# Inverse roots of two norms: Ln and Exp on ScalarE replaced by an addition and a power on GpSimd

## The chip, the cores and the metric

The kernel runs on one core of a Trainium2 chip. The metric is device microseconds of one execution, as the median of several. A core has TensorE (PE in the profile, with its weight loads as PEld), VectorE (DVE), ScalarE (ACT), GpSimd (POOL) and SyncE (SP, which issues most DMAs). Each engine runs its own list of instructions strictly in order, and engines wait for each other with semaphores.

## The reference

Two transformer-like blocks in float32 over 1024 tokens of width 1024, with 16 meta tokens in front. What matters here is the middle of the first block, where two mixers run side by side:

- `hgrn2_mixer` (the recurrence): 6 heads of 64, a gated linear recurrence. Its output `o` is normed for each token and head: `o * rsqrt(mean(o*o) + 1e-6)`, then times a weight and a gate.
- `mamba2_mixer` (the chunks): 6 heads of 64 in 2 groups, done in chunks. Its output `y`, times a gate, is normed for each token over each group of 192: `y * rsqrt(mean(y*y) + 1e-6)`, then times a weight.

After them come a third mixer (already done by then), the output projection, layer norms, two feed-forward parts and a second block, all outside the change.

## The kernel before

The program is written once for each engine (`tensor_program`, `scalar_program`, `vector_program`, `gpsimd_program`, `sync_program`), as a row of stages. The stage of this change is `weave(..._hgrn, ..._ssd)` on each engine. It starts when the projections are done (about 430 us into the span) and ends where the output projection begins (about 716 us).

Each `_hgrn` and `_ssd` function is a Python generator that emits instructions between `yield`s. `weave` takes one step of each generator in turn, hgrn first. So the order of instructions on each engine is fixed when the program is built, by the number of yields, and nothing is reordered on the chip.

- hgrn works on three pairs of heads, i = 0, 1, 2 (`pairs`: at most two live, each starting 9 turns after the one before). A pair runs 17 steps: gates and a scan, the transposes and states, then 7 levels of score products (steps 4 to 12), then the outputs in two halves h = 0, 1 (steps 13 to 16). In steps 13 and 14 ACT copies the outputs of a half out of PSUM and squares them into `S.SQ`. DVE sums the squares for each head into `S.SS[h]` (128x8) in steps 14 and 15 (`squares`), then needs `S.RS[h]`, the inverse root, to scale the outputs (`gated`, steps 15 and 16). PE then transposes them into `YA`.
- ssd works on nine chunks, r = 0 to 8 (`ssd_chunks`: at most two live, chunk r+1 starts in the turn in which chunk r is at step 5, or one earlier). In step 5 DVE finishes `S.Y[x]`, and ACT squares its two groups with an accumulated sum into `S.SSB[x]` (128x2). DVE scales by the inverse root in step 6 (`normed`), and PE transposes it in step 7. Chunk 0 has no norm.

Before the change ACT makes the inverse root itself, with Ln (scale 1/64 or 1/192, bias `k.eps`) and then Exp with scale -0.5: in `root(h)` for the recurrence, in line in `act_ssd` for the chunks. That is 6 roots of 128x8 and 8 of 128x2. The Ln and the Exp are each preceded by a load of an activation table. The other functions of the stage on ACT are Exp, Copy, Relu, Square and Abs, and at the start of a pair one Ln and one Sigmoid.

Behind the root of a chunk in ACT's order stand the decay rows of the next chunk (`gaps`, `decay`), the exponentials of hgrn's levels (`level exp`) and copies of score products out of PSUM, which free the bank in which PE puts the next product.

GpSimd in this stage: `XDD` (128x384, step 1 of a chunk, needed by PE for the state), half of the decayed score product `m2(r, 1)` (128x384, step 3), and per pair the products `QG` (step 1) and `gate` (step 12), both 128x1024. In later stages it makes the roots of the layer norms and of the second block's norm as a power: `g.tt(rs, rs, k.mhalf.to_broadcast(...), ALU.pow)`, with `k.mhalf` a column of -0.5.

Of the kernel before, what the change touches and what calls it, by code (L numbers as in the profile page):

```python
# [9 lines left out]
ALU = mybir.AluOpType  # L10
ACT = mybir.ActivationFunctionType
AX = mybir.AxisListType
ADD, SUB, MUL, MAX, MIN = ALU.add, ALU.subtract, ALU.mult, ALU.max, ALU.min
# [9 lines left out]
RMS_EPS = 1e-6  # L23
# [267 lines left out]
class Kernel:  # L291


    def __init__(self, nc, ctx, A, out, dump=None):
        self.nc, self.A, self.out, self.dumps = nc, A, out, dump or []
        sb = self.sb = Columns(nc, "f", F32, CUTS)
        self.rb = Columns(nc, "r", F32R)
        banks = [ctx.enter_context(nc.psum_tensor(f"bank{i}", [128, 512], F32))[:, :] for i in range(8)]
        L = self.L = Ledger(nc, ctx, banks)
        self.up, self.land, self.past, self.also = L.up, L.land, L.past, L.also  # L300
        self.take, self.bank, self.drain, self.drain2 = L.take, L.bank, L.drain, L.drain2
        R = Region(sb, 0, 53200)
        self.consts = R.take(10 * 128)
        self.ident = self.consts[:, 0:128]
        self.triu = self.consts[:, 128:256]
        self.ones = self.consts[:, 256:384]
        self.lev = [self.consts[:, 384 + 128 * i:512 + 128 * i] for i in range(7)]
        self.P = {}

        self.before = {"m": "o1", "f": "o2"}  # L310
        self.cols = R.take(sum(n for _, n in COLS))
        at = 0
        for n, w in COLS:
            self.P[n] = self.cols[:, at:at + w]
            at += w
        self.rows_at = R.at
        self.rows = R.take(sum(n for _, n in ROWS))

        self.late = sum(n for _, n in ROWS) - 1024
        at = 0  # L320
        for n, w in ROWS:
            self.P[n] = self.rows[:, at:at + w]
            at += w
        self.lnw = R.take(2048)
        self.ring_at = R.at
        self.ring = [R.take(SLOT) for _ in range(4)]
        self.mhalf, self.eps = [v[:, i:i + 1] for v in [R.take(16)] for i in range(2)]
        self.small = R.sub(1022)
        R.at = CUTS[1]
        self.mix = R.sub(8192)  # L330
        self.xt = R.sub(8192 + 128)
        self.work = R.sub(R.b - R.at)

        self.XT = tuple(k8(self.rb[:, at:at + 8 * TM]) for at in (self.xt.a, self.work.b - 8 * TM))
        self.xs = nc.dram_tensor("x_spill", [NT, 1024], F32, kind="Internal").ap()
        self.dr = {n: nc.dram_tensor(n, sh, F32, kind="Internal").ap() for n, sh in (
            ("q_s", [3, 128, NT]), ("f_s", [3, 128, TM]), ("ig_s", [128, 9, 768]),
            ("xb_s", [128, 7, TM]), ("z_s", [128, 8, 384]), ("ac_s", [8, 768]),
            ("gr_s", [8, 4, 128]), ("br_s", [8, 4, 128]))}
        M, W = self.mix, self.work  # L340
        self.x_in = M.sb[:, M.a:M.b].rearrange("p (c d) -> p c d", c=NC)
        self.m_in = W.sb[:, W.a:W.a + 1024][0:NM, :]
        self.YC = M.sb[:, M.a:M.a + 2048].rearrange("p (k t) -> p k t", k=2)
        self.YA, self.YB = (M.sb[:, M.a + o:M.a + o + 3072].rearrange("p (k t) -> p k t", k=3) for o in (2048, 5120))
        self.DTR = self.small.take(54)
        self.c = StageC(self)
        self.a = StageA(self)

        self.H = W.sb[:, W.a:W.a + 8192].rearrange("p (c d) -> p c d", c=NC)
        self.HT = (k8(self.rb[:, self.xt.a:self.xt.a + 8192]), k8(self.rb[:, W.b - 8192:W.b]))  # L350
        sm = self.small
        sm.at = sm.a
        self.lnsm = [(sm.take(12), sm.take(2), sm.take(1)) for _ in range(2)]
        self.o1 = out_panels(self, "w out", self.A["w_out"], [
            (self.ring_at, self.ring_at + SLOT), (self.ring_at + 2 * SLOT, self.ring_at + 3 * SLOT),
            (W.a + 8192, W.a + 8192 + SLOT), (M.a + 4096, M.a + 4096 + SLOT)])
        self.m = StageM(self)
        self.s = StageS(self)
        self.d = StageD(self)
        self.g = StageG(self)  # L360
        self.f = StageF(self)
# [127 lines left out]


def pool_x(k, g):
    g.zero(k.mhalf, -0.5).then_inc(*k.up("half", "half", 0))
    g.zero(k.eps, RMS_EPS).then_inc(*k.up("half", "half"))


def x_done(k, g):
# [793 lines left out]
def act_hgrn(k, g):  # L1290
    S = k.a
    c_done(k, g)
    g.wait_ge(*k.past("half"))

    def one(i):
        KK, G, QG, ST, SM = S.sets[i % 2]
# [64 lines left out]

        OU = [G[:, half_slice(h)] for h in range(2)]

        def root(h):
            g.wait_ge(*k.past("squares", i, h))
            g.act(S.RS[h], S.SS[h], ACT.Ln, scale=1.0 / 64, bias=k.eps).then_inc(*k.up("hgrn acts", "rs ln", i, h))
            g.wait_ge(*k.past("rs ln", i, h))
            g.act(S.RS[h], S.RS[h], ACT.Exp, scale=-0.5).then_inc(*k.up("hgrn acts", "rs", i, h))

        for h in range(2):  # L1370
            if h:
                root(0)
            for p in range(2):
                g.wait_ge(*k.past("o", i, h, p))
                g.cp(OU[h].rearrange("p (c h d) -> p h c d", c=4, h=2)[:, p],
                     k.bank("o", i, h, p)[:, 0:256].rearrange("p (c d) -> p c d", d=64)).then_inc(*k.drain("hgrn acts", "o", i, h, p))
            g.wait_ge(*k.past("drain", "o", i, h, 1))
            if i or h:
                g.wait_ge(*k.past("squares", *((i, 0) if h else (i - 1, 1))))
            g.act(S.SQ, OU[h], ACT.Square).then_inc(*k.up("hgrn acts", "sq", i, h))  # L1380
            yield
        root(1)
        yield
        for h in range(2):
            g.wait_ge(*k.past("ya", i, h))
# [5 lines left out]
def dve_hgrn(k, g):  # L1391
    S = k.a
# [4 lines left out]
    def one(i):  # L1397
# [69 lines left out]
        OU = [G[:, half_slice(h)] for h in range(2)]  # L1467

        def squares(h):
            g.wait_ge(*k.past("sq", i, h))  # L1470
            g.rsum(S.SS[h], S.SQ.rearrange("p (n d) -> p n d", d=64)).then_inc(*k.up("hgrn vec", "squares", i, h))

        def gated(h):
# [23 lines left out]
def pool_hgrn(k, g):  # L1497
    S, P = k.a, k.P
    c_done(k, g)
    g.zero(S.MK, 1.0).then_inc(*k.up("hgrn pool", "mk", 0))  # L1500
    g.wait_ge(*k.past("mk", 0))
    g.zero(S.MK[:, 0:1]).then_inc(*k.up("hgrn pool", "mk", 1))
    g.wait_ge(*k.past("mk", 1))
    g.zero(S.MK[:, NM::128]).then_inc(*k.up("hgrn pool", "mk"))
    for x in range(2):
        g.zero(S.KT[x]).then_inc(*k.up("hgrn pool", "kt zero", x))
        g.wait_ge(*k.past("kt zero", x))
        for p in range(2):
            g.zero(S.QT[x][64 * p:64 * p + 64, :, 1 - p]).then_inc(*k.up("hgrn pool", "qt zero", x, p))
            g.wait_ge(*k.past("qt zero", x, p))  # L1510
    nw = P["hgrn_norm_w"].unsqueeze(1).to_broadcast([128, 16, 64])

    def one(i):
        KK, G, QG, ST, SM = S.sets[i % 2]
        Q, F, V = S.ins[i % 2]
        g3 = S.GT.rearrange("p (n d) -> p n d", d=64)
        yield
        g.wait_ge(*k.past("exp g", i))
        g.wait_ge(*k.past("qv in", i))
        g.tt(QG, QG, Q, MUL).then_inc(*k.up("hgrn pool", "qg", i))  # L1520
        yield
        yield
        yield
        for s in range(9):
            if s == 8:
                g.wait_ge(*k.past("gate in", i))
                g.tt(g3, g3, nw, MUL).then_inc(*k.up("hgrn pool", "gate", i))
            yield
        yield
        yield  # L1530
        yield
    yield from pairs(one)


# [142 lines left out]
def act_ssd(k, g):  # L1677
    S, P, v = k.a, k.P, k.a.v
# [17 lines left out]
    def one(r):  # L1696
        x = r % 2
# [24 lines left out]
        SS = S.SSB[x]  # L1722
        for e in range(2):
            es = slice(192 * e, 192 * e + 192)
            g.act(S.SQB[x][:, es], S.Y[x][:, es], ACT.Square, accum_out=SS[:, e:e + 1]).then_inc(
                *k.up("ssd acts", "y squares", r, e))
        g.wait_ge(*k.past("y squares", r, 1))
        g.act(SS, SS, ACT.Ln, scale=1.0 / 192, bias=k.eps).then_inc(*k.up("ssd acts", "y rs ln", r))
        g.wait_ge(*k.past("y rs ln", r))
        g.act(SS, SS, ACT.Exp, scale=-0.5).then_inc(*k.up("ssd acts", "y rs", r))  # L1730
        yield
        yield
        g.wait_ge(*k.past("yb", r))
# [112 lines left out]
def pool_ssd(k, g):  # L1846
# [6 lines left out]
    def one(r):  # L1853
        x = r % 2
# [13 lines left out]
        g.wait_ge(*k.past("drain", "cb", r))  # L1868
        g.wait_ge(*k.past("decay", r, 1))
        g.tt(e3, e3, bc(S.CB[x][:, 128:256], [128, 3, 128], 1), MUL).then_inc(*k.up("ssd pool", "m2", r, 1))  # L1870
        for _ in range(4):
            yield
    yield from ssd_chunks(one)


# [1688 lines left out]
```

## Time and profile before

| what | value |
|---|---|
| median of 3 runs | 3324.05 us (3318.4 to 3332.33) |
| the profiled execution | 3319.71 us, span 3317.9 us |
| busy in the span: PE, DVE, ACT, POOL | 3044.9, 1427.9, 907.8, 749.6 us |
| chain that ended last, by engine | PE 78%, DVE 11%, ACT 4%, POOL 3%, DMA 2%, issue 2% |
| ACT table loads in the whole span | 84, 107.8 us, 1283 ns each |

The profile records one execution. Busy time of an engine says how much work it has, not whether anyone waits for it. For that the chain is read (the work that ended last, followed back from step to step to what released it), and in the order of time the idle time in front of an instruction with the engine that ended it, written `[idle <-releaser]`. Rows that the trace has merged show a count, and their time is that of the group.

### The profile page before, as it was taken

To read this page: it belongs to the slowest core of one execution; us is meant where nothing else is said; L and a number is where in the kernel's file an instruction comes from. 1 tells how busy PE (TensorE), PEld (TensorE's weight loads), DVE (VectorE), ACT (ScalarE), POOL (GpSimd) and SP (SyncE) were. 2 spreads that over 40 slices of the span, in tenths; PEclk is the share of its full clock that TensorE was granted. 3 is DMA by queue.
4 is the path that set the end of the run, shared out by engine and by line. 5 is a ranking of instruction groups with operands and counts; after the bars stand their busy time and mean duration, and the time that the engine had idled before them with its cause. 6 is when DMAs were issued, how large, how long until landed. Compare 5 with 4: busy or idle time off the path is not lost.

```text
span 3317.9 us, 36176 instructions
## 1 busy us (share of the span) xinstructions
PE 3044.9 (92%) x15317; PEld 2506.5 (76%) x15317; DVE 1427.9 (43%) x2106; ACT 907.8 (27%) x1281; POOL 749.6 (23%) x476
## 2 busy tenths in 40 slices
PE   8889946679999999999999899899999999999997
PEld 7768745567788888888977899766667878777785
DVE  4766547756233333336335255311135433334335
ACT  3211246641211122212246122311112322222221
POOL 0342311103111122213312255201212211111113
PEclk9989966779999999999999999899999999999998
DMA  4112131231111111111211100211121111111111
GB/s 138 58 52 75 45 94 39 61 117 47 43 51 51 48 41 51 51 44 38 82 39 39 58 14 20 77 38 42 48 89 39 39 51 51 38 51 45 44 51 76
DMA packets 152512, 180.46 MB, mean 54 GB/s; under 512 B 6352, under 2 KB 127888, under 8 KB 152352
## 3 DMA queue, kind: packets, MB, share of 16 engines
q1 hardware_dynamic: 143680, 166.51, 16.1%
q10 hardware_dynamic: 8672, 11.65, 1.0%
q8 instruction: 121, 1.98, 0.3%
q14 instruction: 39, 0.32, 0.0%
HBM read 158.05 MB, written 20.09 MB: 54 GB/s over the span
## 4 chain that ended last, share of the span: by engine, by line
PE 78%; DVE 11%; ACT 4%; POOL 3%; DMA 2%; issue 2%; SPq 0%; ACTq 0%; DVEq 0%; POOLq 0%
PE bank L127 76%; DVE f L158 5%; POOL f L158 3%; DVE f L166 2%; ACT f L147 2%; PE bank L142 2%; DVE f L175 1%; ACT L147 1%; DVE r L158 1%; ACT r L150 1%; DMA f<-gr_s 1%; ACT f L150 1%; DVE f L163 1%; DMA f<-x 0%; DMA f<-w_in 0%
## 5 line engine op out<-in xcount | busy, mean ns | idle before, releaser
L127 PE MATMUL bank<-r,r 128*128 128x512 f32 (+4 forms) x11592 | 2453.5, 373 | 46.7 <-DVE r L158 24.4
L127 PEld LDWEIGHTS bank<-r,r 128*128 128x128 f32 x11592 | 2021.7, 190 | 468.5 <-issue 50.9
L158 POOL TENSOR_TENSOR f<-f 128x512 f32<-128x512 f32 (+4 forms) x248 | 330.6, 1339 | 1793.7 <-ACT f L147 642.7
L158 DVE TENSOR_TENSOR f<-f,bank 128x512 f32<-128x512 f32 (+2 forms) x519 | 318.6, 636 | 450.3 <-PE bank L127 448.8
L158 DVE TENSOR_TENSOR r<-f,r 128x512 fp32r<-128x512 f32 (+3 forms) x169 | 228.1, 1357 | 507.9 <-ACT r L150 507.9
L127 PE MATMUL bank<-f 128*128 128x128 f32 (+7 forms) x2344 | 328.8, 306 | 75.4 <-DVE f L158 46.3
L150 ACT ACTIVATE r<-f 128x2048 fp32r<-128x2048 f32 (+2 forms) x217 | 278.8, 1308 | 427.6 <-DMA f<-w_up 183.9
L127 PEld LDWEIGHTS bank<-f 128*128 128x128 f32 (+2 forms) x2344 | 283.3, 203 | 107.4 <-issue 45.7
L166 DVE SCALAR_TENSOR_TENSOR f<-f,f 128x1024 f32<-128x1024 f32 (+3 forms) x169 | 202.4, 1206 | 358.5 <-ACT f L147 330.3
L150 ACT ACTIVATE f<-bank 128x512 f32<-128x512 f32 (+8 forms) x340 | 170.3, 509 | 618.9 <-PE bank L127 560.8
L147 ACT ACTIVATE f<-bank 128x512 f32<-128x512 f32 (+1 forms) x175 | 92.0, 528 | 893.3 <-PE bank L127 889.7
L158 POOL TENSOR_TENSOR r<-f,r 128x2048 fp32r<-128x2048 f32 (+1 forms) x48 | 219.8, 4579 | 443.7 <-ACT r L150 443.7
L127 PE MATMUL bank<-f,f 128*128 128x128 f32 (+6 forms) x788 | 232.3, 460 | 46.8 <-POOL f L158 35.6
L158 POOL TENSOR_TENSOR f<-f,f 128x512 f32<-128x512 f32 (+4 forms) x148 | 194.2, 1325 | 217.4 <-ACT f L147 138.9
L147 ACT ACTIVATE f<-f 128x512 f32<-128x512 f32 (+10 forms) x281 | 175.7, 657 | 181.4 <-DVE f L166 103.8
L127 PEld LDWEIGHTS bank<-f,f 128*128 128x128 f32 (+2 forms) x788 | 130.7, 217 | 119.9 <-issue 81.2
L158 DVE TENSOR_TENSOR f<-bank,f 128x512 f32<-128x512 f32 (+5 forms) x190 | 99.2, 566 | 97.0 <-PE bank L127 51.5
L142 PE MATMUL bank<-f,f 128*128 128x128 f32 (+3 forms) x531 | 85.3, 305 | 50.8 <-DVE f L158 17.7
L158 DVE TENSOR_TENSOR f<-f 64x512 f32<-64x512 f32 (+12 forms) x234 | 122.3, 551 | 16.5 <-ACT f L147 8.9
L142 PEld LDWEIGHTS bank<-f,f 128*128 128x128 f32 (+3 forms) x531 | 69.8, 159 | 59.5 <-DVE f L158 19.3
L147 ACT ACT_TABLE_LOAD x84 | 107.8, 1283 | 9.2 <-DVE f L163 5.8
L150 ACT ACTIVATE r<-bank 128x512 fp32r<-128x512 f32 (+1 forms) x81 | 44.0, 595 | 214.8 <-PE bank L142 214.7
(31 smaller groups left out, 564.4 us busy)
## 6 DMA issues: line engine op xcount, KB each, us to landing
f<-w_in SPq DMA_DIRECT2D x31, 1024.0 KB, 5.5
f<-w_up SPq DMA_DIRECT2D x44, 512.0 KB, 5.2
f<-w_mlp_in SPq DMA_DIRECT2D x16, 1024.0 KB, 5.5
f<-w_mlp_out SPq DMA_DIRECT2D x16, 1024.0 KB, 4.9
f<-w_down SPq DMA_DIRECT2D x11, 1024.0 KB, 5.0
f<-w_out SPq DMA_DIRECT2D x8, 1024.0 KB, 5.1
f<-x_spill SPq DMA_DIRECT2D x4, 2048.0 KB, 10.9
f<-x SPq DMA_DIRECT2D x4, 1024.0 KB, 11.6
```

Source lines behind the costliest of these rows:

```text
L127: return self.g.matmul(out, lhs, rhs, start=start, stop=stop, skip_group_check=True)
L142: return self.g.transpose(out, in_, ident)
L147: return self.g.activation(out, in_, func, **kw)
L150: return self.g.activation(out, in_, ACT.Copy)
L158: return self.g.tensor_tensor(out, a, b, op)
L163: return self.g.tensor_scalar(out, a, s1, s2, op0, op1)
L166: return self.g.scalar_tensor_tensor(out, a, s, b, op0, op1)
L175: return self.g.tensor_tensor_scan(out, d0, d1, init, MUL, ADD)
```

## The change

ACT no longer makes the roots. The divisor of the mean goes into the scale of the square: (0.125 o)^2 is o^2/64, and (192^-0.5 y)^2 is y^2/192. GpSimd adds 1e-6 to the sums, waits for that on its own semaphore, and raises the result to -0.5. In `pool_hgrn` this is put in steps 14 and 15, for the halves 0 and 1; in `pool_ssd` in step 5 of a chunk. DVE waits for the same events `rs` and `y rs` as before, which GpSimd now signals. `squares(h)` on DVE gets a wait for the root of the pair before, since GpSimd reads what it overwrites. The column `k.eps`, its memset, and ACT's wait for it go.

```diff
 def pool_x(k, g):
-    g.zero(k.mhalf, -0.5).then_inc(*k.up("half", "half", 0))
-    g.zero(k.eps, RMS_EPS).then_inc(*k.up("half", "half"))
+    g.zero(k.mhalf, -0.5).then_inc(*k.up("half", "half"))
 def act_hgrn(k, g):
-    g.wait_ge(*k.past("half"))
...
-        def root(h):
-            g.wait_ge(*k.past("squares", i, h))
-            g.act(S.RS[h], S.SS[h], ACT.Ln, scale=1.0 / 64, bias=k.eps).then_inc(*k.up("hgrn acts", "rs ln", i, h))
-            g.wait_ge(*k.past("rs ln", i, h))
-            g.act(S.RS[h], S.RS[h], ACT.Exp, scale=-0.5).then_inc(*k.up("hgrn acts", "rs", i, h))
-
         for h in range(2):
-            if h:
-                root(0)
...
-            g.act(S.SQ, OU[h], ACT.Square).then_inc(*k.up("hgrn acts", "sq", i, h))
+            g.act(S.SQ, OU[h], ACT.Square, scale=0.125).then_inc(*k.up("hgrn acts", "sq", i, h))
             yield
-        root(1)
         yield
 def dve_hgrn(k, g):
         def squares(h):
             g.wait_ge(*k.past("sq", i, h))
+            if i:
+                g.wait_ge(*k.past("rs", i - 1, h))
 def pool_hgrn(k, g):
         yield
-        yield
-        yield
+        for h in range(2):
+            g.wait_ge(*k.past("squares", i, h))
+            g.ts(S.RS[h], S.SS[h], RMS_EPS, None, ADD).then_inc(*k.up("hgrn pool", "rs0", i, h))
+            g.wait_ge(*k.past("rs0", i, h))
+            g.tt(S.RS[h], S.RS[h], k.mhalf.to_broadcast([128, 8]), ALU.pow).then_inc(*k.up("hgrn pool", "rs", i, h))
+            yield
 def act_ssd(k, g):
-            g.act(S.SQB[x][:, es], S.Y[x][:, es], ACT.Square, accum_out=SS[:, e:e + 1]).then_inc(
+            g.act(S.SQB[x][:, es], S.Y[x][:, es], ACT.Square, scale=192.0 ** -0.5, accum_out=SS[:, e:e + 1]).then_inc(
                 *k.up("ssd acts", "y squares", r, e))
-        g.wait_ge(*k.past("y squares", r, 1))
-        g.act(SS, SS, ACT.Ln, scale=1.0 / 192, bias=k.eps).then_inc(*k.up("ssd acts", "y rs ln", r))
-        g.wait_ge(*k.past("y rs ln", r))
-        g.act(SS, SS, ACT.Exp, scale=-0.5).then_inc(*k.up("ssd acts", "y rs", r))
 def pool_ssd(k, g):
-        for _ in range(4):
-            yield
+        yield
+        yield
+        SS = S.SSB[x]
+        g.wait_ge(*k.past("y squares", r, 1))
+        g.ts(SS, SS, RMS_EPS, None, ADD).then_inc(*k.up("ssd pool", "y rs0", r))
+        g.wait_ge(*k.past("y rs0", r))
+        g.tt(SS, SS, k.mhalf.to_broadcast([128, 2]), ALU.pow).then_inc(*k.up("ssd pool", "y rs", r))
+        yield
+        yield
```

## Rows read from the trace of the kernel before

**Rows 1.** Windows: busy us (instructions) of each engine in a stretch, PE clock, DMA.

```profile
485.00:716.00 231.00, 142.62 (x933) 128.19 (x932) 163.40 (x225) 148.85 (x303) 24.91 (x17) 0.73 0.17 51
```

**Rows 2.** Chain, 425 to 730 us: shares by line, first and last load at a root.

```profile
by line: PE bank L127 31.2%; DVE f L158 17.8%; ACT f L147 11.3%; ACT L147 8.0%; issue 6.7%; DVE f L166 3.8%; PE bank L142 3.5%; DVE f L184 3.3%; ACT f L150 2.9%; DMA f<-xb_s 2.7%; DVE f L175 1.5%; DMA f<-ac_s 1.5%; DMA f<-f_s 1.2%; DVE r L1
...
489.39 1.28 ACT L147
...
696.40 1.28 ACT L147
```

**Rows 3.** Groups by shape, ACT, 425 to 730 us: busy, mean ns, idle before.

```profile
L147 ACT ACT_TABLE_LOAD x40 | 51.3, 1283 | 0.7
...
L147 ACT ACTIVATE f<-f 128x2 f32<-128x2 f32 x16 | 4.0, 250 | 0.2
...
L147 ACT ACTIVATE f<-f 128x8 f32<-128x8 f32 x15 | 3.7, 243 | 3.4 <-DVE f L181 3.2
```

**Rows 4.** Timeline around chunk 1's root, 484 to 516 us: start, us, engine.

```profile
489.18 0.19 ACT L147 ACTIVATION_READ_ACCUMULATOR f<-f 128x1 f32 x1
...
492.53 0.75 DVE L166 SCALAR_TENSOR_TENSOR f<-f,f 128x192 f32<-128x192 f32 x2 [0.82 <-ACT f L147]
...
495.76 3.76 PE L127 MATMUL bank<-f,f 128*128 128x128 f32 x16 [5.51 <-ACT f L150]
...
503.95 0.71 DVE L184 COPY_PREDICATED f<-f,bank 128x512 f32<-128x512 uint32 x1 [1.34 <-PE bank L127]
```

**Rows 5.** Timeline around chunk 2's root, 505 to 542 us.

```profile
508.77 0.89 PE L127 MATMUL bank<-f 128*128 128x192 f32 x4 [1.19 <-POOL f L158]
...
511.36 3.75 PE L127 MATMUL bank<-f 128*128 128x128 f32 x16 [1.70 <-DVE f L184]
...
519.44 1.24 DVE L166 SCALAR_TENSOR_TENSOR f<-f,f 128x1040 f32<-128x1040 f32 x1 [7.62 <-ACT f L147]
```

**Rows 6.** Timeline at the roots of chunks 4, 6, 7 and 8.

```profile
583.10 0.75 DVE L166 SCALAR_TENSOR_TENSOR f<-f,f 128x192 f32<-128x192 f32 x2 [0.51 <-ACT f L147]
...
654.01 4.59 DVE L158 TENSOR_TENSOR f<-f 128x512 f32<-128x512 f32 x6 [1.88 <-ACT f L147]
...
657.32 1.07 ACT L150 ACTIVATE f<-bank 128x512 f32<-128x512 f32 x2
...
680.74 0.75 DVE L166 SCALAR_TENSOR_TENSOR f<-f,f 128x192 f32<-128x192 f32 x2 [0.75 <-ACT f L147]
...
682.74 3.52 DVE L158 TENSOR_TENSOR f<-f 64x512 f32<-64x512 f32 x2 [0.32 <-ACT f L147]
...
692.43 4.78 PE L127 MATMUL bank<-f 64*128 64x64 f32 x32 [1.38 <-DVE f L184]
...
697.80 0.64 ACT L150 ACTIVATE f<-bank 128x256 f32<-128x256 f32 x2
```

**Rows 7.** Timeline at the root of chunk 5, 600 to 658 us.

```profile
614.33 2.44 DVE L184 COPY_PREDICATED f<-f,bank 128x512 f32<-128x512 uint32 x2 [2.56 <-PE bank L127]
```

**Rows 8.** Groups by shape, POOL, whole span.

```profile
L158 POOL TENSOR_TENSOR f<-f 128x1 f32<-128x1 f32 x40 | 22.0, 550 | 267.8 <-DVE f L163 267.7
L158 POOL TENSOR_TENSOR f<-f,f 128x256 f32<-128x256 f32 x16 | 11.9, 753 | 45.3 <-ACT f L147 45.3
...
L158 POOL TENSOR_TENSOR f<-f 128x4 f32<-128x4 f32 x8 | 8.1, 1011 | 64.0 <-DVE f L163 64.0
L158 POOL TENSOR_TENSOR f<-f,f 128x384 f32<-128x384 f32 x7 | 6.3, 894 | 69.0 <-ACT f L147 39.7 <-DVE f L158 24.9 <-ACT f L150 4.4
...
L172 POOL MEMSET f<- 128x2 f32 x4 | 0.2, 100 | 2.8 <-DVE f L166 2.8
```

**Rows 9.** Timeline of a later stage, DVE and POOL, 803 to 819 us.

```profile
804.82 2.60 DVE L166 SCALAR_TENSOR_TENSOR f<-f,f 128x1024 f32<-128x1024 f32 x2 [0.66 <-POOL f L158]
...
818.08 4.62 POOL L158 TENSOR_TENSOR r<-f,r 128x2048 fp32r<-128x2048 f32 x1
818.15 5.64 DVE L166 SCALAR_TENSOR_TENSOR f<-f,f 128x1024 f32<-128x1024 f32 x1 [1.15 <-POOL f L158]
```

More of the change, by code:

```diff
@@ L326, in __init__ @@
         self.ring = [R.take(SLOT) for _ in range(4)]
-        self.mhalf, self.eps = [v[:, i:i + 1] for v in [R.take(16)] for i in range(2)]
+        self.mhalf = R.take(16)[:, 0:1]
         self.small = R.sub(1022)
```

## The prediction

> **What bounds the kernel now.** I first read the page. TensorE is busy for 92% of the span and carries most of the chain that ended last; that part of the kernel has no norm of this kind in it and doesn't change. So I read the stage by itself. In its 231 us from the first root to the output projection, PE is busy 143 us, DVE 163, ACT 149 and POOL 25 [rows 1]. No engine bounds it: it is a ring of short waits, in which each engine now and then is the last. The chain through the stage has table loads of ACT at 8.0% of 305 us, some 24 us [rows 2]. Walking down that list, 14 of them are loads before a root's Ln or Exp, two each at the roots of chunks 1, 2, 4, 6, 7 and 8 and at the second root of pair 1; the first stands at 489.39, the last at 696.40 [rows 2]. That is 18.0 us of 1.283 us each, and with the Ln and Exp behind them some 21 us of the chain. The reader should see that ACT's roots lie on the path, but also that the neighbours' idle times beside them are mostly much shorter than the 3 us that a root takes.
>
> **What goes away.** Each of 14 roots has two loads and two small activations. Of the 40 loads in the stage [rows 3] 28 go, since without the Ln everything that stands around a root is in the set of Exp, or needs no set of its own; 12 stay (the first ones, and those of the pairs' Ln and Sigmoid). 28 x 1.283 = 35.9 us, 16 x 0.250 = 4.0 us and 12 x 0.243 = 2.9 us: ACT loses 42.8 of its 149 us. One root costs ACT 2 x 1.283 + 2 x 0.25, about 3.05 us: chunk 1's accumulator read ends at 489.37, and DVE's `normed` starts at 492.53 [rows 4].
>
> The Trainium skill ("ScalarE: Activation LUTs", What ACT_TABLE_LOAD costs) puts a drain of about 1380 ns beside the 1283 ns of each switch. In the chain the load begins at 489.39, 0.02 us behind the read that ends at 489.37 [rows 2, 4], so no such drain shows; by the page the 14 loads of the chain would be worth 19.3 us more. I give it no chance of its own.
>
> **What is added.** On POOL 14 additions and 14 powers. The power is on record for one and four columns: 550 and 1011 ns [rows 8], that is 154 ns for each column on 396 ns. An estimate from that is 0.70 us for two columns and 1.63 us for eight; bounds are 0.55 to 1.01 us for two, and 1.01 us to twice that for eight. An addition of this form isn't in the trace. The nearest from below is a memset of 128x2, 0.10 us; from above the power of one column, 0.55 us. The elementwise products of 256 and 384 columns, 753 and 894 ns [rows 8], leave 0.47 us when drawn down to no columns, so I take 0.45 us. With handoffs of under 0.1 us, a chunk's root is ready some 1.3 us after its squares instead of 3.1 us, a half's some 2.2 us after its sum. POOL gains 8 x 1.15 + 6 x 2.08 = 21.7 us on 25. The scales in the squares, the missing memset and the lost wait for `half` cost and give nothing: an immediate operand, and a start that nobody waits for. DVE's new wait for a root of the pair before is met tens of us earlier.
>
> **Where it pays.** At each root I ask who is late next, if ACT runs 3.05 us earlier.
>
> - Chunk 1. DVE loses its idle 0.82 us before `normed`. PE had waited 5.51 us for ACT's copy of a score product, starts 3 us earlier, and takes away DVE's next idle, 1.34 us [rows 4]. After that DVE has no gap left of any size: 2.2 us.
> - Chunk 2. Behind the root ACT prepares pair 1's gates, for which DVE waits 7.62 us [rows 5]. Nothing else is near: the whole 3.05 us.
> - Chunk 4. DVE is idle 0.51 us [rows 6] and then itself sets PE's start: 0.6 us.
> - Chunk 6 and pair 1's second root. DVE's wait of 1.88 us goes. But what leads on is ACT's copy of pair 1's last half at 657.32 [rows 6], which lets SP issue the next loads; before it ACT has to wait for a score product of PE that hardly moves: 0.8 us of a possible 1.88.
> - Chunk 7. DVE is idle 0.75 and 0.32 us: 1.07 us.
> - Chunk 8. ACT's next work copies outputs that PE ends at 692.43 + 4.78 = 697.21; it copies at 697.80 [rows 6]: 0.6 us.
> - The others give nothing. At chunk 5 DVE waits 2.56 us for PE, not for ACT [rows 7]; at chunk 3, both roots of pair 0, the first of pair 1 and both of pair 2, ACT stands waiting for PE's outputs or DVE for other work of its own.
>
> Sum 2.2 + 3.05 + 0.6 + 0.8 + 1.07 + 0.6 = 8.3 us of the 21 us on the chain.
>
> **What it costs.** First the queue. POOL takes chunk r's root before `XDD` of chunk r+1 when r is even (2, 4, 6), so `XDD` starts after ACT's squares and the root, some 1.5 us later. PE waits for it at chunk 2, 1.19 us, but then again 1.70 us for DVE [rows 5]: the delay fits. The other two have wider gaps. I take nothing here, with 1 us as the bound. If that cover were gone each place would cost up to 1.5 us.
>
> Second, the two engines disturb each other. In a later stage a two-input DVE operation starts 0.07 us after a GpSimd product of 4.62 us and takes 5.64 us, where its like takes 1.30 us [rows 9]: it was held until GpSimd was through. The Trainium skill ("GPSIMD Engine Reference", Key points) says so: the two share their interfaces to SBUF, and a DVE instruction with two SBUF inputs contends. By that rule the change puts 21.7 us of holding instructions beside a DVE that is busy 71% of the stage; the trace agrees for products, and has no DVE operation under a power.
>
> Seven roots fall where DVE works without a pause behind them (chunks 1, 4, 6, 7, the second roots of all pairs, less their gaps). If DVE were held for all of it, 4 x 1.15 + 3 x 2.08 = 10.8 us. An operation of 0.6 us in flight isn't disturbed, and some read PSUM: I take 0.35 us for a chunk's root and 1.0 us for a pair's, 4 x 0.35 + 3 x 1.0 = 4.4 us. The ends are 0 and 10.8 us.
>
> Net -8.3 + 4.4 = -3.9 us. Against the profiled execution, 3319.71 us, that is 3315.8 us; this execution lies 4.3 us below the median of the runs shown, 3324.05 us, and at that the sum gives 3320 us. I forecast 3317 us, between the two. What a measurement of this kernel can tell from no change is about 0.5%, 16.6 us: below 3307.4 or above 3340.7 us. So the forecast is no change that can be told, on the fast side.
>
> **Rivals.**
>
> - The whole chain pays. If ACT were the last at every one of the seven places, 7 x 3.05 = 21.3 us go and the time is 3303 us. For it: the list of the chain. Against it: the idle times of DVE beside it, 0.82, 0.51, 0.75 us, which show DVE right behind. Pieces of it could come back, since an ACT with 43 us less work answers sooner everywhere. Chance 0.16.
> - GpSimd holds DVE (the other side). Place: the seven roots above; price: 10.8 us against a gain of 8.3, so 2.5 us slower, 3327 us. It decides once the held time passes 8.3 of the 21.7 us added. For it: rows 9. Against it: a power is mostly computing on few columns. Chance 0.17, almost all of it still within 0.5%.
> - The loads stay or move: the loads that go here come back before another function, and nothing changes but 3 us of activations. Against it: no other Ln lies near a root. Chance 0.03; 3321 us.
> - The clock. PE is granted 0.73 of full speed in the stage [rows 1]. That lies between its two levels, 1.2 and 2.4 GHz. Sixteen score products took 3.76 us [rows 4]; if such a burst comes at the other level, that is worth up to 1.9 us either way, and four of them 7.5 us. It has no sign that I can give, and widens the range. Chance 0.04 that it decides.
>
> **The numbers.** The forecast, a gain of 0 to 12 us, has 0.60; the rivals have the 0.40 above. Faster by over 0.5%: most of the first rival and a little of the clock and of the forecast's end, 0.15. Slower by over 0.5%: only holding and clock together, 0.03. Within: 0.82. The range goes from the first rival, 3303 us, less 2 us for what that leaves out, to the second, 3327 us, and 1 us for the spread of the runs: 3301 to 3328 us.
>
> **What would show it.** Right: 56 table loads in the span, 12 in the stage; ACT busy some 865 us, POOL some 771; a power of 128x2 near 0.7 and of 128x8 near 1.6 us; DVE's `normed` with no wait before it at chunks 1, 4 and 7; `log f` of pair 1 some 5 us earlier; the output projection starting 4 us earlier; all behind it shifted alone. Wrong: DVE operations of two or three times their length under the powers at the seven places, PE waits above 2 us for `XDD`, or a stage shorter by over 12 us.

## The result, and the profile after

| kernel | median | runs | range |
|---|---|---|---|
| before | 3322.24 us | 20 | 3316.38 to 3332.33 |
| after | 3313.51 us | 20 | 3306.12 to 3320.63 |

The ratio is 0.997, 95% interval 0.9961 to 0.9978: 7.3 to 13.0 us faster, 8.7 us by the medians. That is less than the 0.5% (16.6 us) that the prediction took as its bound, and with 20 runs of each kernel it is still told from zero: the bound was too wide. The forecast was 3317 us, in a range of 3301 to 3328. In the profiled executions the output projection starts at 709.54 us and not at 716.53, 7.0 us earlier, where 4 were forecast.

The page of the kernel after: the span, the busy times and the chain by engine.

```profile
span 3311.0 us, 36150 instructions
...
PE 3048.0 (92%) x15317; PEld 2509.6 (76%) x15317; DVE 1428.5 (43%) x2106; ACT 865.3 (26%) x1225; POOL 777.7 (23%) x503
...
PE 78%; DVE 11%; POOL 3%; ACT 3%; issue 2%; DMA 2%; SPq 0%; ACTq 0%; DVEq 0%; POOLq 0%
```

ACT has 42.5 us less than its 907.8, as forecast (865). POOL has 28.1 us more than its 749.6, where 21.7 were forecast. The chain by engine says nearly nothing at this size. The stretch from chunk 1's root to the output projection does (windows of the kernel after, columns as in [rows 1]):

```profile
485.20:709.50 224.30, 145.10 (x933) 130.86 (x932) 163.12 (x226) 107.19 (x247) 54.10 (x45) 0.72 0.18 54
```

Against [rows 1]: the same work in 6.7 us less, ACT 149 to 107 us, POOL 25 to 54, and DVE 163.40 to 163.12. The last pair is the first answer to the question that the prediction left widest. GpSimd's 28 new instructions made DVE's work in the stage no longer.

POOL's groups by shape, whole span, kernel after: the new instructions.

```profile
L158 POOL TENSOR_TENSOR f<-f 128x8 f32<-128x8 f32 x6 | 11.8, 1966 | 0.5
L158 POOL TENSOR_TENSOR f<-f 128x2 f32<-128x2 f32 x8 | 7.7, 961 | 0.7
L162 POOL TENSOR_SCALAR f<-f 128x8 f32<-128x8 f32 x6 | 5.4, 899 | 23.4 <-DVE f L181 23.2
L162 POOL TENSOR_SCALAR f<-f 128x2 f32<-128x2 f32 x8 | 3.5, 438 | 84.1 <-ACT f L147 84.1
```

And ACT's table loads, 425 to 722 us, where [rows 3] had 40:

```profile
L147 ACT ACT_TABLE_LOAD x12 | 15.4, 1283 | 0.2
```

**Where the time came from.** I put both kernels on one clock that starts with the first 128x1040 activation of the stage (433.30 us before, 433.58 after), and took the time from the start of each chunk's first square to that of the next one's. Each kernel was profiled more than once: before_again is a second execution of the kernel before, after_again and after_third_b are a second and a third of the kernel after.

| stretch, from a chunk's squares on | predicted gain | before, us | before_again | after | after_again | after_third_b |
|---|---|---|---|---|---|---|
| chunk 1 to 2 | 2.2 | 18.6 | 19.3 | 16.0 | 15.9 | 16.0 |
| chunk 2 to 3 | 3.05 | 44.1 | 44.1 | 40.8 | 41.0 | 41.0 |
| chunk 3 to 4 | 0 | 27.9 | 31.2 | 30.4 | 28.1 | 28.3 |
| chunk 4 to 5 | 0.6 | 32.6 | 32.5 | 29.2 | 29.3 | 29.3 |
| chunk 5 to 6 | 0 | 33.7 | 37.3 | 33.7 | 33.9 | 34.0 |
| chunk 6 to 7 | 0.8 | 31.3 | 31.7 | 32.0 | 30.6 | 32.0 |
| chunk 7 to 8 | 1.07 | 17.2 | 17.0 | 15.3 | 15.6 | 15.3 |
| chunk 8 to the output projection | 0.6 | 22.6 | 23.7 | 23.4 | 22.6 | 23.4 |
| all of it | 8.3 | 228.0 | 236.8 | 220.8 | 216.9 | 219.3 |

Four places pay in all three executions of the kernel after, against either of before: chunks 1, 2, 4 and 7. In the mean, and against the first execution of before, that is 2.7 + 3.2 + 3.4 + 1.8 = about 11 us. The other lines differ as much between two executions of one kernel (3.3 and 3.6 us at chunks 3 and 5 before, 2.3 and 1.4 us at chunks 3 and 6 after); at chunk 3 that difference is the clock's (last section). With these lines counted the whole is 7.2, 11.1 and 8.7 us shorter than the first execution of before.

The places as the trace of after shows them, chunk 1 first.

```profile
489.65 0.30 POOL L162 TENSOR_SCALAR f<-f 128x2 f32<-128x2 f32 x1 [5.69 <-ACT f L147]
490.03 1.01 POOL L158 TENSOR_TENSOR f<-f 128x2 f32<-128x2 f32 x1
...
491.82 0.74 DVE L166 SCALAR_TENSOR_TENSOR f<-f,f 128x192 f32<-128x192 f32 x2
...
492.82 2.77 PE L127 MATMUL bank<-f,f 128*128 128x128 f32 x16 [2.36 <-ACT f L150]
...
501.81 1.29 DVE L184 COPY_PREDICATED f<-f,bank 128x512 f32<-128x512 uint32 x2
...
513.87 1.24 DVE L166 SCALAR_TENSOR_TENSOR f<-f,f 128x1040 f32<-128x1040 f32 x1 [4.93 <-ACT f L147]
```

The root is ready at 491.04, before DVE is free, and `normed` has no wait. PE waits 2.36 us for ACT's copy and not 5.51 [rows 4]. DVE's wait of 1.34 us before the pick (`COPY_PREDICATED`, which takes a score product out of PSUM) is gone. At 513.87 `log f` of pair 1 (DVE's first operation on its gates) waits 4.93 us and not 7.62 [rows 5]; on the common clock it starts at 80.3 and not at 86.1, 5.8 us earlier, where I had said "some 5".

Chunk 4, where the prediction had 0.6 us:

```profile
576.84 0.74 POOL L162 TENSOR_SCALAR f<-f 128x2 f32<-128x2 f32 x1 [10.67 <-ACT f L147]
577.67 1.12 POOL L158 TENSOR_TENSOR f<-f 128x2 f32<-128x2 f32 x1
...
578.77 0.86 POOL L158 TENSOR_TENSOR f<-f,f 128x384 f32<-128x384 f32 x1
578.86 1.31 DVE L166 SCALAR_TENSOR_TENSOR f<-f,f 128x192 f32<-128x192 f32 x2
...
579.78 2.85 PE L127 MATMUL bank<-f 128*128 128x192 f32 x20 [2.30 <-POOL f L158]
...
583.27 1.88 DVE L184 COPY_PREDICATED f<-f,bank 128x512 f32<-128x512 uint32 x2
```

These are the rows of before for the same work; [rows 6] has only its first line, at 583.10.

```profile
586.72 3.75 PE L127 MATMUL bank<-f 128*128 128x128 f32 x16 [5.40 <-ACT f L150]
...
588.80 1.03 DVE L184 COPY_PREDICATED f<-f,bank 128x512 f32<-128x512 uint32 x1 [1.61 <-PE bank L127]
...
590.50 1.01 DVE L184 COPY_PREDICATED f<-f,bank 128x512 f32<-128x512 uint32 x1 [0.68 <-PE bank L127]
```

Before, PE's products stood 5.40 us for ACT's copies out of PSUM, which stood behind the root. DVE then waited 1.61 and 0.68 us for those products. After, both waits are gone. So DVE's gaps at this root were 0.51 + 1.61 + 0.68 = 2.80 us, of which I had counted the first. The stretch lost 3.4 us; the 0.6 us between the two are not traced.

At chunk 7 too DVE waited for PE behind the two gaps that I had counted. The rows of before:

```profile
687.73 3.31 PE L127 MATMUL bank<-f,f 128*128 128x128 f32 x16 [2.12 <-DVE f L184]
...
689.38 1.30 DVE L184 COPY_PREDICATED f<-f,bank 128x512 f32<-128x512 uint32 x1 [0.65 <-PE bank L127]
...
691.08 1.29 DVE L184 COPY_PREDICATED f<-f,bank 128x512 f32<-128x512 uint32 x1 [0.41 <-PE bank L127]
```

And the products in the kernel after:

```profile
680.94 2.22 PE L127 MATMUL bank<-f,f 128*128 128x128 f32 x16 [0.73 <-DVE f L184]
```

DVE's 0.65 and 0.41 us for PE have shrunk to 0.16 us. PE waits less and does the same 16 products in 2.22 us and not 3.31.

**PE's clock went with the loads.** That last difference is the granted clock, 0.57 of full speed before and 1.00 after, and it recurs. In the four profiles with the chunks' loads on ACT (before, before_again, and the experiments pairs_only and after_loads) PE waits 4.8 to 5.5 us before the 16 products behind chunk 1's root and does them in 3.43 to 3.76 us, at a clock of 0.50 to 0.57. In the eight without, it waits 1.7 to 3.1 us and takes 2.02 to 3.50 us. At chunk 4 they took 3.62 to 3.76 us with the loads (clock 0.50 to 0.54), and 2.13 to 3.10 us in the seven of the eight that have the same products in the same place. So PE's waits behind the loads and its slower products come together, and no run here parts them. What can be read is that the gain doesn't follow the length of these products once the loads are gone: at chunk 1 they took 2.77, 2.02 and 3.50 us in the three executions of after, at chunk 4 2.13, 2.78 and 2.88, and the stretches are equal within 0.15 us.

### The profile page after: what moved, and what is told of

Same layout as the page of the kernel before. It is cut to its first block, busy times and chain, and to the rows that moved or that the text cites. A ratio compares the mean times of both kernels' runs of the same rounds, so it can differ in the third digit from the quotient of the medians.

```text
span 3311.0 us, 36150 instructions
## 1 busy us (share of the span) xinstructions
PE 3048.0 (92%) x15317; PEld 2509.6 (76%) x15317; DVE 1428.5 (43%) x2106; ACT 865.3 (26%) x1225; POOL 777.7 (23%) x503
## 4 chain that ended last, share of the span: by engine, by line
PE 78%; DVE 11%; POOL 3%; ACT 3%; issue 2%; DMA 2%; SPq 0%; ACTq 0%; DVEq 0%; POOLq 0%
PE bank L127 77%; DVE f L158 5%; POOL f L158 3%; DVE f L166 2%; PE bank L142 2%; DVE f L175 1%; ACT f L147 1%; DVE r L158 1%; ACT r L150 1%; DMA f<-gr_s 1%; DVE f L163 1%; ACT f L150 1%; DVE f L184 0%; DMA f<-x 0%; DMA f<-w_in 0%
## 5 line engine op out<-in xcount | busy, mean ns | idle before, releaser
L158 POOL TENSOR_TENSOR f<-f 128x512 f32<-128x512 f32 (+5 forms) x262 | 349.8, 1341 | 1709.0 <-ACT f L147 609.9
L147 ACT ACTIVATE f<-f 128x1024 f32<-128x1024 f32 (+9 forms) x253 | 168.7, 702 | 195.3 <-DVE f L166 103.9
L142 PEld LDWEIGHTS bank<-f,f 128*128 128x128 f32 (+3 forms) x531 | 70.0, 159 | 59.2 <-DVE f L158 18.6
L158 DVE TENSOR_TENSOR f<-f,f 128x512 f32<-128x512 f32 (+3 forms) x116 | 92.6, 851 | 4.2 <-DMA f<-wsp 2.3
```

What stands on the lines that cost most here:

```text
L142: return self.g.transpose(out, in_, ident)
L147: return self.g.activation(out, in_, func, **kw)
L158: return self.g.tensor_tensor(out, a, b, op)
```

## The experiments

Each was timed in turn with the kernel before, and its ratio is to that kernel. Diffs are against the kernel after.

**chunks_only**: the recurrence's roots are ACT's again (Ln and Exp), the chunks' stay on GpSimd.

```diff
 act_hgrn:  + root(0) ahead of half 1's copies, root(1) behind its squares (Ln, Exp)
 pool_hgrn: - both additions and powers
```

> Only the chunks' eight roots are on GpSimd; the pairs' six stay on ScalarE as before the change. Theory A (ScalarE's time at the chunks' roots is what was gained, and the pairs' roots lie where ScalarE waits anyway): nearly the whole gain of the full change, 6 to 9 us faster than before, the only loss a wait of about 2 us before DVE's scaling of pair 1's last half. Theory B (what matters is how much work ScalarE loses in all): about half of the gain goes, since 12 of the 28 loads come back: 4 us faster. The start of the output projection, 716.5 us before and 709.5 us after the change, would be near 710 by A and near 713 by B.

Measured: 0.997 [0.9961, 0.9979], 3312.15 us. **pairs_only** is the opposite half.

```diff
 act_ssd:  + g.act(SS, SS, ACT.Ln, scale=1.0 / 192, bias=k.eps); + g.act(SS, SS, ACT.Exp, scale=-0.5)
 pool_ssd: - addition and power
```

> Only the pairs' six roots are on GpSimd; the chunks' eight stay on ScalarE. Theory A: 0 to 2 us faster than before, output projection starts at 715 to 716 us, and table loads before roots still stand in the chain. Theory B: 3 to 4 us faster.

Measured: 1.0001 [0.999, 1.0012], 3321.87 us beside 3322.36. The chunks' eight roots give all of the gain, and the recurrence's six give none that can be told (the interval leaves 3 to 4 us either way), though the six take 6 x 3.05 = 18 us off ACT. This is the cleanest case here of work that costs nothing where it stands. The other sign that I had named failed: the output projection starts at 717.6 us in the trace of chunks_only, where 710 was expected, and at 718.9 in that of pairs_only, where it was 715 to 716. The profiled execution of chunks_only took 3320.38 us, the longest of its 12; at chunks 1, 2 and 4 its stretches are 15.9, 41.0 and 29.3 us, as in the kernel after, and the time went at chunks 3 and 5 (31.1 and 37.3 us), where before_again has lost it too. The medians decide here.

**no_root**: GpSimd makes nothing new. The addition and the power are left out, and DVE scales by the sum of the squares itself, so the norm is not computed.

```diff
 squares (DVE):  - wait for the root of the pair before
 gated (DVE):    - wait ("rs", i, h), factor S.RS[h]    + wait ("squares", i, h), factor S.SS[h]
 normed (DVE):   - wait ("y rs", r)                     + wait ("y squares", r, 1)
 pool_hgrn, pool_ssd:  - additions and powers
```

> As the changed kernel, but the addition and the power are left out: VectorE scales by the sum of squares itself, so GpSimd gets none of the 14 roots and nobody waits for them. Theory A (GpSimd's new work is hidden): like the changed kernel, the output projection within 1 us of its 709.5 us, apart from bursts of products that come at another clock. Rival C (GpSimd's new work holds VectorE or comes late, and eats part of the gain): 3 to 5 us faster than the changed kernel, 705 us.

Measured: 0.9971 [0.996, 0.9982], 3310.81 us. It isn't told apart from after (0.9961 to 0.9978), though the two intervals leave room for some 4 us. The trace is sharper: were DVE held by the new instructions, its busy time would fall without them. In 224 us from 485 on it is 163.83 us here, with 25.61 us of POOL, and 162.82 us in the kernel after, with 54.10. These windows don't cut both stages at the same operation. Over the same 224 DVE operations, from the first root's stretch to the output projection, DVE is busy 163.2 us before, 162.5 in the kernel after and 162.6 here. The prediction's 4.4 us of held DVE are not there.

```profile
485.00:709.00 224.00, 143.50 (x939) 128.99 (x938) 163.83 (x227) 107.20 (x248) 25.61 (x17) 0.74 0.18 53
```

**after_loads**: the roots stay on GpSimd, and ACT gets its loads back at the chunks, with an Ln and an Exp of one column that nobody waits for.

```diff
 def act_ssd(k, g):
+        g.act(S.idle, k.mhalf, ACT.Ln, scale=-1.0, bias=k.eps).then_inc(*k.up("ssd acts", "idle", r, 0))
+        g.wait_ge(*k.past("idle", r, 0))
+        g.act(S.idle, k.mhalf, ACT.Exp, scale=-0.5).then_inc(*k.up("ssd acts", "idle", r, 1))
```

> The changed kernel, and ScalarE still does an Ln and an Exp of one column on a scratch value behind each chunk's squares, each with its table load, for which nobody waits. It gives ScalarE's time back and leaves the root on GpSimd. Theory A: the gain of the chunks' part goes, within 2 us of before: 3320 to 3324 us, output projection near 716 us. If instead the gain came from the root being ready sooner for VectorE (3.1 us before, some 1.7 us now), most of it stays: 3315 us.

Measured: 1.0007 [0.9998, 1.0017], 3323.51 us beside 3322.36: the gain is gone, and at its places: the stretches of chunks 1, 2, 4 and 7 take 17.8, 43.9, 32.4 and 17.5 us. Around chunk 1 in its trace:

```profile
491.29 1.14 POOL L158 TENSOR_TENSOR f<-f 128x2 f32<-128x2 f32 x1
...
492.08 1.28 ACT L147 ACT_TABLE_LOAD   x1
492.49 0.74 DVE L166 SCALAR_TENSOR_TENSOR f<-f,f 128x192 f32<-128x192 f32 x2
...
496.84 3.43 PE L127 MATMUL bank<-f,f 128*128 128x128 f32 x16 [4.82 <-ACT f L150]
```

The root itself is early and DVE starts `normed` with no wait; but PE again stands 4.82 us for the copy behind the loads. At chunk 4 DVE's 0.51 us before `normed` is gone too, and its 1.61 and 0.68 us for PE are back. Over the stage PE waits 15.6 us for such copies before, 5.1 us after, and 10.6 us here. The reader should see which half of the change works. That the root comes sooner is worth nothing measurable (the interval leaves at most 0.7 us of gain). That ACT isn't stopped for 3 us in front of its next work (the copies, and at chunk 2 the gates of pair 1) is worth all of it.

**pool_triple**: behind each power two more of the same size, to a buffer that nobody reads, so 28 more powers.

```diff
 pool_hgrn, pool_ssd, behind the root:
+            for n in range(2):
+                g.tt(idle, sums or ones, k.mhalf.to_broadcast([128, 8 or 2]), ALU.pow), and a wait for it
```

> The changed kernel, and behind each power GpSimd does two more powers of the same shape on a scratch value, for which nobody waits: eight times two of 128x2 and six times two of 128x8, 1.0 and 2.0 us each as the changed kernel's trace has them, some 40 us more in the stage. If VectorE is held while GpSimd does a power, DVE's group times grow by up to a third of that, 5 to 13 us more. If it is not held, only the products queued behind come late: XDD of chunks 3, 5 and 7 by 2 us each and the power of pair 1's second half by 2 us; 0 to 4 us slower than the changed kernel.

Measured: 0.9981 [0.9969, 0.9992], 3319.57 us beside 3325.7. In 224 us from 485 on POOL is busy 85.84 us and DVE 162.82:

```profile
485.00:709.00 224.00, 143.73 (x939) 129.33 (x937) 162.82 (x224) 104.95 (x245) 85.84 (x73) 0.75 0.18 52
...
576.42 4.22 POOL L158 TENSOR_TENSOR f<-f 128x2 f32<-128x2 f32 x3
...
580.72 0.83 POOL L158 TENSOR_TENSOR f<-f,f 128x384 f32<-128x384 f32 x1
...
581.70 4.11 PE L127 MATMUL bank<-f 128*128 128x192 f32 x20 [5.47 <-POOL f L158]
...
584.95 1.91 DVE L184 COPY_PREDICATED f<-f,bank 128x512 f32<-128x512 uint32 x2 [2.85 <-PE bank L127]
```

Some 32 us more of powers (40 were expected) leave DVE's busy time where it was; over the same 224 operations it is 163.1 us. What they cost, 0.11% or some 4 us by the middle values (the intervals overlap), comes through the queue: `XDD` stands behind them, PE waits 5.47 us for it, and DVE 2.85 us for PE. The stretches of chunks 4 and 6 take 32.2 and 35.0 us, 3 us more each than in the kernel after, and those of chunks 1, 2 and 7 no more. This is the wait for which the prediction had 0, with up to 1.5 us for each place if its cover were gone.

**xdd_first_b**: is a piece of that wait already in the kernel after? Its PE waits 3.42 us at chunk 2 and 2.30 us at chunk 4 for `XDD`, above the 2 us that the prediction had named as a sign of being wrong. The root of chunks 2, 4 and 6 goes behind it.

```diff
 pool_ssd:
-        (root of chunk r in step 5)
+        if r in (2, 4, 6): keep the root, and issue it behind XDD of chunk r + 1
```

> The kernel after, with the root of chunks 2, 4 and 6 issued on GpSimd behind the copy of the next chunk's X instead of ahead of it. If what the vector engine waits for at these chunks is the copy (it is late by the root's GpSimd time), the tensor engine's waits for GpSimd in the stage fall from 5.7 us to about 2 us and the kernel is 1 to 3 us faster than the kernel after. If what is late there is the vector engine's own work or the root itself, the time stays within 1 us of the kernel after, and the wait turns up at the chunk's normed squares.

**after_third_b**: the kernel after, unchanged, timed in turn with it.

> The kernel after, unchanged, as the neighbour of the run above on the same chip: 0.3% faster than the kernel before, the stage 272 to 280 us long from the scalar engine's first activation in it.

Measured: 0.9966 [0.9953, 0.9978], 3312.99 us, against 0.9968 [0.9957, 0.998], 3311.92 us. PE's waits for GpSimd fell from 5.7 to 1.2 us in the stage, and the medians are 1 us apart. Chunk 4 of this run:

```profile
580.18 0.74 DVE L166 SCALAR_TENSOR_TENSOR f<-f,f 128x192 f32<-128x192 f32 x2
...
581.26 2.23 PE L127 MATMUL bank<-f 128*128 128x128 f32 x16 [2.28 <-ACT f L150]
```

These products end 6.66 us after the start of the squares (576.83 to 583.49), in the kernel after also 6.66 (575.97 to 582.63). ACT's copies were right behind `XDD`. So the row named POOL, and taking POOL away bought nothing: the release that came last hid another right before it. The wait wasn't at the chunk's normed squares either, as the expectation's second case had it; it was ACT's. One other thing differs in this trace, as it does in that of chunks_only: at chunk 7 PE waits 2.12 us, as before the change, and takes 3.1 us for its 16 products, and the stretch is 16.1 us and not 15.3.

**filled**: matmuls of the identity in PE's idle time ahead of the transposes of pairs 1 and 2 and of the pairs' outputs, to keep the clock up.

```diff
 def fill(b, n): n times g.mm(b[:, 0:128], k.ident, k.ident)
 ahead of the transposes of pairs 1, 2:  + fill(b, 12)
 ahead of a pair's outputs:              + fill(bb[0], 3, 7 or 2)
```

> The changed kernel with TensorE kept busy in the idle time before its transposes and outputs: identity products into a bank that it holds already and overwrites, 12 before the transposes of pairs 1 and 2, and 3, 7 and 2 before the outputs of pairs 0, 1 and 2. If part of the gain was lost to bursts at 1.2 GHz, such as pair 0's outputs (15.00 us after the change, 12.14 before), the bursts behind the fill come at 2.4 GHz and the stage is 5 to 12 us shorter than the changed kernel's 276 us, 3303 to 3309 us. If the clock plays no part, the fill gives nothing, or costs up to 3 us where it ends late.

Measured: 0.996 [0.9944, 0.9975], 3313.83 us beside 3325.7. It isn't told apart from after, and it isn't the 3303 to 3309 us that a gain by the clock should have given. The clock from 485 to 709 us rose from 0.73 to 0.77, but the outputs of pair 0 stayed at the low level:

```profile
539.69 15.58 PE L127 MATMUL bank<-f 128*128 128x128 f32 x77 [2.33 <-DVE f L166]
```

Whether a better fill would pay stays open. **after_again** and **before_again** are one more execution of each kernel, for a second profile.

> The changed kernel once more, for a second trace: how much of the stage's length, 276.0 us from the first activation to the output projection in the first trace, comes out of the clock. If the clock's levels fall differently from run to run, the stage differs by 1 to 4 us, and all of it in PE's bursts; the idle times of DVE and ACT at the roots stay.

> The kernel before once more, for a second trace of its stage: 283.2 us in the first. Differences of 1 to 4 us in PE's bursts, with the same waits at the roots.

Measured: 3311.81 and 3335.23 us. From the stage's first activation to the output projection 272.20 and 292.27 us; the first pair of executions had 275.96 and 283.23. The two executions of before lie 9 us apart in this stage, where 1 to 4 were expected, those of after 3.8 us, so a single pair may show anything from 7 to 20 us.

## Why the prediction was right, and where its terms were off

- **"28 of the 40 loads go, ACT loses 42.8 us."** 12 stay, ACT is at 865.3 us. Right. So was the root's price: the two ways to the 3.05 us of a root (loads and activations; the gap from read to `normed`) are borne out at chunk 2, where ACT is last and 3.1 to 3.3 us came. By the Trainium skill ("ScalarE: Activation LUTs", What ACT_TABLE_LOAD costs), with its drain of 1.38 us at each load, an estimate for such a place is 5.8 us (3.05 and two drains); the trace doesn't agree.
- **"Where it pays", 8.3 us.** The direction and the choice of places were right, the sizes partly. Chunk 1: 2.2 against 2.6 to 2.8. Chunk 2: 3.05 against 3.1 to 3.3. Chunk 7: 1.07 against 1.6 to 1.9; in xdd_first_b and chunks_only, where PE waits 2.12 us there as before, it is 1.1, so the rest hangs on PE's shorter wait and faster products. Chunk 4 is the term that was mis-sized: 0.6 (for a gap of 0.51) against 3.4. The prediction's sentence was that DVE "then itself sets PE's start". It didn't. PE stood 5.40 us for ACT, and DVE's gaps for PE, 1.61 and 0.68 us, were ACT's as well, at one remove. I had counted only gaps whose row names ACT. At chunk 1 I had followed the same path and found its 1.34 us. Chunk 6, 0.8 us, didn't show (31.3 and 31.7 us before, 30.6 to 32.0 after). Nor did chunk 8, 0.6 us; a burst at a lower clock lay over it in all three executions (32 matmuls in 5.62 to 6.44 us against 4.78 [rows 6], which took 6.74 in before_again).
- **"It was held until GpSimd was through", -4.4 us.** This step failed. DVE's busy time in the stage is 163.2 us before, 162.6 without the new work, 162.5 with it and 163.1 with three powers for each one. The few DVE operations that stretched lie under `XDD` and other elementwise products, as before: `normed` of chunk 4 took 1.31 us (578.86) and not 0.74. The 0.35 and 1.0 us that the term gave to each root stood on no row, and no run shows them. It is the other way round, see the last section. That is also why POOL's 21.7 us came out at 28.1: a power of 128x2 took 0.96 us in the mean and not 0.70, one of 128x8 1.97 and not 1.63, and an addition of 128x8 0.90 and not 0.45.
- **"The queue": nothing, bound 1 us.** Right for the time, and the sign that I had named for being wrong (a wait for `XDD` above 2 us) was a bad one. It came (3.42 us at chunk 2), and it was covered: moving it away gave nothing.
- **Rivals.** The whole chain pays, 21.3 us: no, the interval ends at 13.0. GpSimd holds DVE: no. The loads stay: no. The clock: left open. I gave it no sign, but the burst that I named (3.76 us [rows 4]) was at the lower level already (0.50) and could only get shorter, and so it did; how much of the difference of medians is the clock's isn't shown, and it decides what two single profiles look like.

Gains of about 11 us at four places, less nothing for the holding, against 7.3 to 13.0 measured: the account closes within what the executions differ by. My net of 3.9 us is less than half of the 8.7 measured. It had two errors that added up, 2.8 us at chunk 4 and 4.4 us for the holding, against 1.4 us that chunks 6 and 8 didn't give. That 3317 us still lies near 3313.51 is in part luck: the forecast was put between two bases, 3319.71 and 3324.05 us, and that took 3 us more off the second than the sum gives.

## What to carry to other kernels

Ask of an engine in the middle of a ring not when its result is needed but what stands behind it in its queue: here an earlier root alone gave nothing, and ACT's earlier work behind it, copies out of PSUM above all, gave everything. When gaps are added up for such a change, follow them one engine further: a DVE that waits for PE, which waits for ACT, is waiting for ACT. And a wait put down to one engine is worth only the distance to the next release, so try it by moving the work before you count it.

## What the runs showed of the hardware that was not expected

**The small GpSimd instruction gives way, not DVE.** Rows of the kernel after, a power alone at first and then beside DVE operations (spans on POOL are rough in this profile, but these agree within 0.01 us in the other executions of the kernel):

```profile
606.08 0.23 POOL L162 TENSOR_SCALAR f<-f 128x2 f32<-128x2 f32 x1 [5.41 <-ACT f L147]
606.39 0.71 POOL L158 TENSOR_TENSOR f<-f 128x2 f32<-128x2 f32 x1
...
642.41 2.46 POOL L158 TENSOR_TENSOR f<-f 128x8 f32<-128x8 f32 x1
...
672.30 1.14 POOL L158 TENSOR_TENSOR f<-f 128x2 f32<-128x2 f32 x1
...
692.75 2.28 DVE L158 TENSOR_TENSOR r<-f,r 128x2048 fp32r<-128x2048 f32 x1
692.92 2.22 POOL L162 TENSOR_SCALAR f<-f 128x8 f32<-128x8 f32 x1 [4.89 <-DVE f L181]
695.22 1.65 POOL L158 TENSOR_TENSOR f<-f 128x8 f32<-128x8 f32 x1
...
700.91 2.06 POOL L158 TENSOR_TENSOR f<-f 128x8 f32<-128x8 f32 x1
701.37 2.29 DVE L158 TENSOR_TENSOR r<-f,r 128x2048 fp32r<-128x2048 f32 x1
```

A power takes 0.71 us for two columns and 1.65 for eight where DVE leaves it alone, which are the 0.70 and 1.63 of the prediction's line through [rows 8]. Beside a busy DVE it takes up to 1.14 and 2.46 us. The addition of 128x8 that began 0.17 us into a DVE product of 2.28 us ended with it, after 2.22 us, where one with DVE nearly at rest (at 548.45) took 0.25. The rows follow one pattern. Nine powers of the kernel after began while a DVE `TENSOR_TENSOR` was running, and each ended 0.57 to 0.59 us (two columns) or 1.51 to 1.52 us (eight) after that operation's end, as if it had waited for it. With the large product of [rows 9] it was DVE that stood still. The Trainium skill ("GPSIMD Engine Reference", Key points) has GpSimd contend for SBUF with a DVE instruction that has two SBUF inputs; the trace agrees that the two hold each other up. Which of them pays isn't settled by who came first alone. At 692.75 DVE came first and GpSimd paid; in [rows 9] and at 578.77, where `normed` stretched to 1.31 us, a GpSimd product came first and DVE paid. But behind a power DVE doesn't pay: the product of 701.37 began 0.46 us into one and took 2.29 us, as the like one of 692.75 took 2.28, and none of the 15 DVE operations of the stage that began during a power is more than 0.01 us longer than in no_root. Why a product holds DVE and a power doesn't is open.

**The clock of one and the same burst differs between executions.** Pair 0's outputs, 72 matmuls behind a wait of 2.42 us: 12.14 us in the profile of before, 15.00 in that of after, and 11.90 in after_again and after_third_b, whose program is the same as after's. Windows over the second part of the burst, after and then after_again, the clock being the third figure from the end:

```profile
543.50:552.30 8.80, 8.80 (x41) 7.49 (x40) 3.80 (x5) 4.42 (x14) 3.73 (x4) 0.50 0.00 1
```

```profile
545.00:550.50 5.50, 5.50 (x37) 4.54 (x37) 3.80 (x5) 3.62 (x11) 2.95 (x4) 0.78 0.01 1
```

Both bursts begin at full clock and fall to 0.50, which is 1.2 GHz, within 2 us. In the one it stays there to the end. In the other it is at 0.50 from 540.6 to 547.3 us and at 1.00 again from 547.4 to 550.7. That is 3.1 us in one burst, as much as a whole root, and the line "chunk 3 to 4" of the table shows 2.3 us of it as a loss of the change that isn't one. At this size a single pair of profiles tells where waits went, and not how long the stage is.
